# Attention on one Trainium2 core: causal masks and forget sums as 64-row products, and a group's four output products issued together

## The reference, cut to what matters

```python
def fox_attention(q, k, v, log_f):          # first block, 8 heads of 64
    c = jnp.cumsum(log_f, axis=-1)
...
        s = jnp.einsum('bhqd,bhkd->bhqk', qi, k) * scale
        s = s + ci[..., :, None] - c[..., None, :]
        s = jnp.where(kpos[None, :] <= qpos[:, None], s, -jnp.inf)
        p = jax.nn.softmax(s, axis=-1)
        return jnp.einsum('bhqk,bhkd->bhqd', p.astype(v.dtype), v)
```

## Time and profile before

| | |
|---|---|
| Time, median of 3 runs | 3448.42 us (3446.2 to 3449.67) |
| Span of the profiled execution | 3446.9 us |
| Its own time | 3446.9 us, since nothing is counted outside the span |
| PE busy | 3242.4 us (94%), 15918 matmuls |
| DVE busy | 1296.3 us (38%) |
| ACT busy | 958.9 us (28%) |
| Causal stage, layer 1 and layer 2 | 256 to about 397 us, 1093 to 1240 us of the span |
| MLA stage | 1895 to 1963 us |
| GQA stage | 2691 to 2804 us |

### The profile page before, as it was taken

The page is one execution under the profiler, slowest core; times in us unless marked ns, Lnnn a source line. Parts: engine busy times, 40 slices in busy tenths (PEclk is TensorE's granted clock), DMA queues, the critical chain, the costliest instruction groups (busy, mean ns, idle before and its releaser), DMA issues. The chain is left out here.

```text
span 3446.9 us, 39641 instructions
## 1 busy us (share of the span) xinstructions
PE 3242.4 (94%) x15918; PEld 2176.3 (63%) x15918; DVE 1296.3 (38%) x1781; ACT 958.9 (28%) x1570; POOL 238.9 (7%) x377
## 2 busy tenths in 40 slices
PE   7999999999999999999997999999988999999996
PEld 5885578887787567888785466444436556544442
DVE  4315554242522564333366472111116656111112
ACT  3325433132322533323242431000004543000001
POOL 1004200000101410000000200000000320000000
PEclk9999999999999999999997999999999999999999
DMA  5410122321540022222311216999992112799997
GB/s 156 129 43 24 64 87 94 98 93 57 137 127 32 1 86 86 98 92 92 89 36 23 86 56 257 422 424 424 424 417 75 61 62 93 304 423 424 424 424 303
DMA packets 234149, 590.12 MB, mean 171 GB/s; under 512 B 42690, under 2 KB 146184, under 8 KB 184852
## 3 DMA queue, kind: packets, MB, share of 16 engines
q1 hardware_dynamic: 234004, 588.08, 45.1%
HBM read 581.75 MB, written 2.10 MB: 169 GB/s over the span
## 5 line engine op out<-in xcount | busy, mean ns | idle before, releaser
L2579 PE MATMUL ps<-w_ring,xe 128*64 128x512 f32 x1024 | 235.9, 604 | 5.0 <-PEq L119 5.0
L422 DVE TENSOR_TENSOR mlp_w_lo<-w_ring,mlp_w_hi 128x2048 fp32r<-128x2048 f32 x62 | 142.1, 2292 | 212.7 <-ACT mlp_w_hi L382 212.7
L357 PE MATMUL ps<-h_hi,in_w_hi 128*128 128x512 f32 (+1 forms) x528 | 207.0, 392 | 2.1 <-DVE h_lo L430 2.1
L357 PE MATMUL ps<-h_hi,in_w_lo 128*128 128x512 f32 (+1 forms) x528 | 205.6, 389 | 0.0
L357 PE MATMUL ps<-h_lo,in_w_hi 128*128 128x512 f32 (+1 forms) x528 | 205.6, 389 | 0.0
L357 PE MATMUL ps<-h_hi,mlp_w_hi 128*128 128x512 f32 x512 | 202.6, 396 | 2.1 <-DVE h_lo L430 2.1
L357 PE MATMUL ps<-h_hi,mlp_w_lo 128*128 128x512 f32 x512 | 202.5, 396 | 0.0
L357 PE MATMUL ps<-h_lo,mlp_w_hi 128*128 128x512 f32 x512 | 202.5, 395 | 0.0
L357 PE MATMUL ps<-mlp_w_hi,u_lo 128*128 128x512 f32 x512 | 202.3, 395 | 0.0
L357 PE MATMUL ps<-mlp_w_hi,u_hi 128*128 128x512 f32 x512 | 202.2, 395 | 0.0
L357 PE MATMUL ps<-mlp_w_lo,u_hi 128*128 128x512 f32 x512 | 202.2, 395 | 0.0
(11 more groups left out here) (560 smaller groups left out, 6480.5 us busy)
## 6 DMA issues: line engine op xcount, KB each, us to landing
w_ring<-in_w SPq DMA_DIRECT2D x192, 1024.0 KB, 12.4
ex_front<-in_w SPq DMA_DIRECT2D x96, 1024.0 KB, 12.8
ex_back<-in_w SPq DMA_DIRECT2D x96, 1024.0 KB, 13.0
w_ring<-in_w_in SPq DMA_DIRECT2D x32, 1024.0 KB, 5.4
w_ring<-in_w_up SPq DMA_DIRECT2D x32, 1024.0 KB, 5.5
w_ring<-in_w_down SPq DMA_DIRECT2D x32, 1024.0 KB, 5.0
w_ring<-in_cmp_w SPq DMA_DIRECT2D x16, 512.0 KB, 5.0
w_ring<-in_w_out SPq DMA_DIRECT2D x8, 1024.0 KB, 6.0
```

The source lines that it names most:

```text
L357: mm = pe.matmul(ps[0:o.rows, bank[k], 0:o.cols], lhsT, rhs, start=(o.first and j == 0), stop=(o.final and j == len(o.mm) - 1))
L422: dve.tensor_tensor(w.lo[:, home(n), 0:used], ring.slots[:, n % RING, 0:used], w.hi[:, home(n), 0:used].bitcast(F32), ALU.subtract).then_i ...
L2579: mm = pe.matmul(ps[rows, bank + half, :], lhsT, slot(2 * m + a)[:, kk, 512 * half:512 * half + 512], start=(k == 0), stop=(k == DC - 1))
```

## The change

Three things change in `attention` and one in what feeds it. The mask is now four products of 64 rows and 64 columns a unit, two for each head, from a table `later` of 128 x 320 (two stationary tables of 128 columns and a moving one of 64): the first pair covers the first 64 of the last 128 keys, the second the others. The forget sum is a product of 64 rows for each head, from that head's half of `sel` and `negc`; `negc` therefore holds its rows twice, which DVE writes with two more instructions. mix(g, 0) to mix(g, 3) all stand in step 4g + 7, ahead of flip(4g + 4), and keep(g) in step 4g + 8 instead of 4g + 11, for all four stages. The start loads `later` (160 KB for 64 KB), half of `ones` (32 KB less) and a small table `heads`, from which `sel` is now a copy.

```diff
-                    for a in range(2):
-                        if kind == "causal":
-                            more.append((a, C.ident_r[:, :], C.tri_neg[:, :], n - P, n))
+                    if kind == "causal":
+                        for half in range(2):
+                            for a in range(2):
+                                later = C.later[HD * a:HD * a + HD, :]
+                                more.append((a, later[:, P * half:P * half + P], later[:, 2 * P:], n - P + HD * half, n - P + HD * half + HD))
...
-                    u = step - LAG - 1 - (TT - 1)
-                    if 0 <= u < nu:
-                        mix(u // TT, u % TT)
+                    g, i = divmod(step - LAG - TT, TT)
+                    if 0 <= g < len(groups) and i == 0:
+                        for kb in range(TT):
+                            mix(g, kb)
...
-                    u = step - LAG - 2 - (TT - 1)
-                    if u >= 0 and u % TT == TT - 1:
-                        keep(u // TT)
+                    g, i = divmod(step - LAG - TT - 1, TT)
+                    if 0 <= g < len(groups) and i == 0:
+                        keep(g)
...
-                        dve.tensor_tensor(cmp.sel[:, :, :], C.ident[:, 0:H1].unsqueeze(2).broadcast_to([P, H1, P]),
-                                          C.ident[:, LO:LO + H1].unsqueeze(2).broadcast_to([P, H1, P]), ALU.add).then_inc(s.sel_made, 1)
+                        dve.tensor_copy(cmp.sel[:, :, :], C.heads.unsqueeze(2).broadcast_to([P, H1, P])).then_inc(s.sel_made, 1)
...
-                                        bias=lambda a, n, c=c: (sel[:, 2 * c + a, :], negc[:, 0:n]), gate=None, cmp=None, sharp=None))
+                                        bias=lambda a, n, c=c: (sel[rows(a), 2 * c + a, :], negc[rows(a), 0:n]), gate=None, cmp=None, sharp=None))
...
         c.link(dve.tensor_scalar(negc[0:H1, :], ft[:, 0, :], -1.0, None, ALU.mult))
-        dve.scalar_tensor_tensor(negc[LO:LO + H1, :], ft[:, 0, :], -1.0, negc[0:H1, :].bitcast(F32), ALU.mult, ALU.subtract).then_inc(s.f_done, 1)
+        dve.tensor_scalar(negc[HD:HD + H1, :], ft[:, 0, :], -1.0, None, ALU.mult)
+        dve.scalar_tensor_tensor(negc[LO:LO + H1, :], ft[:, 0, :], -1.0, negc[0:H1, :].bitcast(F32), ALU.mult, ALU.subtract)
+        dve.scalar_tensor_tensor(negc[HD + LO:HD + LO + H1, :], ft[:, 0, :], -1.0, negc[0:H1, :].bitcast(F32), ALU.mult, ALU.subtract).then_inc(s.f_done, 1)
```

More of the change, by code:

```diff
@@ L2778, in build @@
         columns = sb("columns", [P, 32])
-        C = Names(ident=sb("ident", [P, P]), ones=sb("ones", [P, P]), cmp_row=columns[:, 0:1], eps=columns[:, 1:2], rstd=columns[:, 4:8],
-                  norm_st=columns[:, 8:24].rearrange("p (a t) -> p a t", a=4),
+        C = Names(ident=sb("ident", [P, P]), ones=sb("ones", [P, HD]), cmp_row=columns[:, 0:1], eps=columns[:, 1:2], rstd=columns[:, 4:8],
+                  norm_st=columns[:, 8:24].rearrange("p (a t) -> p a t", a=4), heads=columns[:, 24:32],
                   **{n: ctx.enter_context(sbuf(nc, n, shape, F32R)) for n, shape in
-                     (("ident_r", [P, P]), ("tri_neg", [P, P]), ("cmp_neg", [P, TT, 32]))})
-        tri, cmp = ring.slots[:, 0, 0:P], ring.slots[:, 1, 0:P].rearrange("p (t n) -> p t n", t=TT)
+                     (("ident_r", [P, P]), ("later", [P, 2 * P + HD]), ("cmp_neg", [P, TT, 32]))})
+        tri, cmp = ring.slots[:, 0, 0:2 * P + HD], ring.slots[:, 1, 0:P].rearrange("p (t n) -> p t n", t=TT)
         load(nc, "ld", [(x[:, :, :], I["x"][0].rearrange("(t p) n -> p t n", p=P)), (C.ident[:, :], I["c_ident"]),
-                        (C.ones[:, :], I["c_ones"]), (tri, I["c_tri_neg"]), (cmp, I["c_cmp_neg"]),
-                        (C.cmp_row[:, :], I["c_cmp_row"]), (C.eps[:, :], I["c_eps"])])
+                        (C.ones[:, :], I["c_ones"][:, 0:HD]), (tri, I["c_later"]), (cmp, I["c_cmp_neg"]),
+                        (C.cmp_row[:, :], I["c_cmp_row"]), (C.eps[:, :], I["c_eps"]), (C.heads, I["c_heads"])])
         with stage(nc, "ct", "copied") as (block, s):
@@ L2790, in _ @@
             def _(act):
-                for dst, src in ((C.ident_r[:, :], C.ident[:, :]), (C.tri_neg[:, :], tri), (C.cmp_neg[:, :, :], cmp)):
+                for dst, src in ((C.ident_r[:, :], C.ident[:, :]), (C.later[:, :], tri), (C.cmp_neg[:, :, :], cmp)):
                     act.activation(dst, src, ACT.Copy).then_inc(s.copied, 1)
@@ L2821, in constants @@
     c = {"c_ident": np.eye(P), "c_ones": np.ones((P, P)), "c_eps": np.full((P, 1), EPS),
-         "c_tri_neg": np.where(q[None, :] > q[:, None], NEG, 0.0)}
+         "c_heads": q[:, None] % LO == np.arange(H1)[None, :]}
+    r, row, last = q[:, None] % HD, q[None, :], q[:, None] % HD == HD - 1
+    first, second = (row == r) & ~last, np.where(last, row < HD, row == HD + r)
+    c["c_later"] = np.concatenate([first, second, np.where(last | (row[:, 0:HD] > r), NEG, 0.0)], 1)
     end = np.arange(32) * CMP_STRIDE + CMP_BLOCK - 1
```

## The result

| | before | after |
|---|---|---|
| Time, median | 3446.9 us | 3469.2 us |
| Ratio | | 1.0059 (95%: 1.0043 to 1.0075) |
| Profiled execution, its own time | 3446.9 us | 3473.0 us |
| PE busy | 3242.4 us (94%) | 3216.1 us (93%) |

The forecast was 3463, with a range of 3452 to 3475. PE is busy 26 us less and the kernel takes 21 us more. The two profiled executions differ by 24.3 us of span. By stage, from the first scores to the last mix: causal -3.9 (layer 1) and -5.4 (layer 2), MLA +5.1, GQA +27.2; the start +0.8, the stretch between the two causal stages +3.3 (its matmuls begin at half clock), all others together -2.8.

What follows compares the result with a forecast made beforehand. PE's own time was taken to bound the causal stages, a chain through three engines GQA. GQA +17.7, MLA +4.3, causal -7.8, start +0.4 and `sel` -0.4 make +14.2 on the median 3448.4: 3463 us, range 3452 to 3475.

Steps and rivals of the forecast that it cites:

- The bound and the chain: GQA: PE waits for a chain through three engines, 7.07 us against 6.51 before; the stage gets +17.7 us.
- the walk: The prediction's step-by-step timing of the engines through a group; in GQA 15.66 us a group against 13.03.
- rival B: GQA: the clock falls in the new waits, some 1.7 us each time, +12 us, 3475; chance 0.10.
- The mixes that follow are dense: GQA: the prediction's argument against the clock falling in the new wait of 2.5 us a group.
- MLA: MLA groups 15.9 us for 15.0, PE waiting 1.1; +0.9 twice and +2.55 at the end, +4.3 us.
- Causal: Causal stages: groups 10.2 us with forget sums, 9.85 and 10.85 without; -7.8 us in all, between -14 and +1.
- Masks: Causal units: 0.16 us gained each without forget sums; with them 0.27 to 0.40, 1.27 a group.
- rival C: Causal masks: the heads do not run side by side in the small products; +8 us, 3471; chance 0.08.
- Mixes: Four mixes together take 3.58 us for 4.04, in causal groups 2.30 for 2.76; 0.46 saved per group.
- Rival A: All stages: PE's time is what counts, so 35 us faster, 3413; chance 0.11.
- The rest: Start +0.4 us for more loading; two more DVE instructions for `negc` cost nothing; `sel` as a copy -0.4.

Runs made afterwards that it cites:

- the filler: The whole change plus two unread 64-row products in GQA's wait ahead of the flip of i2; 3462.5 us, ratio 1.0046 to the kernel before.
- experiment 5: The whole change with keep(g) back in step 4g + 11; 3457.0 us, ratio 1.0027 to the kernel before.
- halves_grouped: The change's masks and grouped mixes, keep in step 4g + 11, each take split between ACT and DVE by head; 3415.4 us, ratio 0.9901 to before.
- Experiment 10: The same run as halves_grouped: grouped mixes with each take split between ACT and DVE by head; 3415.4 us, ratio 0.9901 to before.
- masks_only: The change's masks and forget sums, with mixes and keeps in the steps of the kernel before; 3427.7 us, ratio 0.9952 to before.
- after_swap: The whole change with takes exchanged: ACT takes i0 and i3, DVE i1 and i2; 3482.6 us, ratio 1.0105 to the kernel before.
- keep_late: The same run as experiment 5: the whole change with keep(g) back in step 4g + 11; 3457.0 us, ratio 1.0027 to before.

## Why the prediction was right, point by point

- **The bound and the chain.** Right. With the filler, GQA has six distances of 15.48 for 15.66, and the last distance is 2.06 longer (12.96 for 10.90) where the walk has +2.1. The last burst takes another 1.3 (4.38 for 3.05, to its last product), which is half clock and not the chain. In all +18.2, of it +16.9 by the chain, for +17.7.
- **The clock (rival B).** Wrong. The prediction names a fall of the clock in GQA's waits as a sign that it is wrong, and the clock fell there. It came on top of the forecast, which had left it out with a chance of 0.10. Its price was +9.0 us in GQA (119.2 to 110.2 with the filler) for the 12 worked out, 1.2 to 1.5 behind each wait for 1.7, and 1.6 more in MLA's last burst. That the time lies in the range all the same owes something to the range, whose upper end is B's 3475; the profiled execution, 3473, is nearer to B than to the forecast. "The mixes that follow are dense" was no argument against it: the clock fell behind the wait all the same, and the mixes came after. The Trainium skill ("TensorE: Matmul & The Clock Gate", "HAM oscillation — how this bites in real kernels") tells of a kernel in which each burst starts at the low clock again after a wait for a DMA; the trace agrees that such falls repeat (0.52 behind the wait above), here with waits for a copy.
- **MLA.** +4.3 was right in sum (+5.1), by two errors. The groups cost +0.53 instead of +0.9. The walk's own terms (6.7 + 2.75 + 2.75 + 3.6) add up to 15.8, not 15.9; the flip of i2 came 6.58 behind that of i0 for 6.7, and the rest of a group took 8.97 for 9.1. The keep was not in that chain, which begins with PE's scores (experiment 5). The end is +4.1 instead of +2.55: the last distance is +2.57, as forecast, and the last burst +1.57 (5.22 for 3.65) at half clock.
- **Causal.** Forecast groups 10.2, 9.85, 10.85; measured 10.23, 9.81, 10.79. Ahead of the first mix -1.6 in layer 1 for -1.7. The walk's chain without a keep adds up to 2.75 by its terms, where it says 3.0. Both stages -9.3 for -7.8, and that is partly luck: layer 2 has -5.7 ahead of its first mix, where it spent 10 us at half clock for 17, and its last burst gave 2.0 back (4.33 for 2.37).
- **Masks.** Mask alone: 0.16 a unit was right as a mean (0.67 a group, 10.98 to 10.31), though it comes as 0.23 in three units and nothing in the fourth; in halves_grouped, where that take is early, the fourth gains 0.23 too (1.20 from scores to mix). Forget sums with it: 1.55 a group for 1.27. The heads run side by side, so rival C is out.
- **Mixes.** A burst costs 3.59 and 2.31, as forecast (3.58, 2.30).
- **Rival A**, PE's time decides. Out. PE's busy time did fall, by 26 us, and the kernel got slower. The Trainium skill ("TensorEngine Tiling (Array Packing)", "Key Properties") says that a change of tiling mode drains the engine; the trace agrees, with 3.59 for four mixes in a row and 4 x 1.01 for four apart. That is PE's time, and here the waits spent it. Experiment 10 takes nearly all of the waits away in GQA and MLA, and even there the stages stay as long as ungrouped (MLA +0.2, GQA -0.1).
- **The rest.** The start +0.8 for +0.4. The +3.3 between the causal stages was not foreseen. It is half-clock time (14 us in the stretch for 7), but the waits at the stage's end are not its cause: masks_only, whose last waits are those of before, has half clock in the same place too (3.4 us, behind the same wait of 3.43 that the kernel before has). Why the kernel before has none there is open.

Open: how much of the median's 21 us is clock. Runs of one kernel differ by up to 20 us (after_swap, 3476 to 3495). The two profiled executions of masks_only differ by 11.6, of which 7.9 lie between the second causal stage and MLA (647.4 and 655.3), which the change doesn't touch.

## What to carry to other kernels

When you move work on a busy engine, ask what it covered where it stood: each mix hid one take, and four mixes in one place hide one. Price a regrouping by walking the other engines' chain between two of the engine's waits, for each stage, with the queue order of every engine in it; three changes of mode (0.15 us each) are soon lost to one bare wait. Shorten the hidden chain first, and then group: the order of the two decides if the grouping costs. And read a small gain from the distances in the stage, not from the medians alone, which carry half-clock time from elsewhere.

## What the runs showed of the hardware

- In GQA the clock fell to 1.2 GHz behind five of six idle waits of 2.3 us (the change) and behind two of six waits of 1.7 (keep_late). Two unread products of 64 rows in the gap (1.88 us) kept it at 2.4 GHz there, and GQA was 9 us shorter.
- The two heads' products of 64 rows ran side by side in all the sizes here, 64 columns too: from its scores to its mix a 128-key unit with a forget sum takes 0.24 + 0.44 (masks_only), where it took 0.42 + 0.60 with forget sum and mask of 128 rows.
